# First expert's 128 rows placed by their ranks, both of its passes ahead of the sorted tiles; last token tile routed from plain rows; weighted sum at the end by diagonal matrices

## The reference

```python
x = x + gate1 * (jnp.concatenate([y_ssm, y_g], axis=-1) @ lp['w_out'])
h2 = _rmsnorm(x, lp['norm2_w']) * (1.0 + scale2) + shift2
moe_out = _moe(h2.reshape(-1, D_MODEL), router_w, router_b, lp['w_gate'], lp['w_up'], lp['w_down'])
x = x + gate2 * moe_out.reshape(x.shape)
y = _rmsnorm(x, final_norm_w)
```

## Time and profile before

| what | value |
|---|---|
| median of three runs (lowest, highest) | 549.62 us (546.81, 556.56) |
| the profiled execution | 547.45 us |
| its span | 545.7 us |
| TensorE busy | 470.6 us (86%) |
| VectorE busy | 238.7 us (44%) |
| ScalarE busy | 147.9 us (27%) |
| GpSimd busy | 102.3 us (19%) |
| moved by DMA | 164.62 MB, mean 302 GB/s |
| mean granted TensorE clock | 0.949 |

### The profile page before, as it was taken

How to read it: one execution, slowest core, us unless ns; L and a number is a source line. 1 busy time by engine, 2 the same in 40 slices (tenths; PEclk the granted TensorE clock), 3 DMA queues, 4 the chain that set the end, 5 groups by cost and what they waited for, 6 DMA issues and landing times. The chain is left out here.

```text
span 545.7 us, 8907 instructions
## 1 busy us (share of the span) xinstructions
PE 470.6 (86%) x3241; PEld 230.4 (42%) x3242; DVE 238.7 (44%) x589; ACT 147.9 (27%) x284; POOL 102.3 (19%) x182
## 2 busy tenths in 40 slices
PE   2788989899969999982888999999998999999960
PEld 1125669655559644462352333233333333333320
DVE  2698994999963300766664101111011101111067
ACT  3545794532147610231030010100001100111242
POOL 3000150988870203500500000000000000000400
PEclk9977999999999999985799999999999999999995
DMA  8992046449497999110797999999999999999922
GB/s 286 340 401 98 1 154 216 165 166 343 140 390 290 347 410 415 73 70 1 272 415 284 380 422 386 392 420 417 418 421 419 407 416 420 417 420 421 409 89 115
DMA packets 42475, 164.62 MB, mean 302 GB/s; under 512 B 3242, under 2 KB 4010, under 8 KB 32580
## 3 DMA queue, kind: packets, MB, share of 16 engines
q1 hardware_dynamic: 35440, 144.22, 67.3%
q10 hardware_dynamic: 4580, 11.91, 5.6%
q0 software_dynamic: 2416, 7.98, 3.8%
HBM read 152.76 MB, written 11.34 MB: 301 GB/s over the span
## 5 line engine op out<-in xcount | busy, mean ns | idle before, releaser
L728 PE MATMUL psum<-arena 128*64 128x512 f32 x672 | 149.1, 595 | 14.0 <-PEq L760 11.0
L728 PEld LDWEIGHTS psum<-arena 128*64 128x64 f32 x672 | 49.7, 137 | 99.5 <-issue 95.0
L741 PE MATMUL psum<-arena 128*64 128x512 f32 x336 | 76.1, 593 | 1.9 <-DVE arena L1594 1.6
L1589 DVE TENSOR_TENSOR arena<-arena,psum 128x256 f32<-128x256 f32 x21 | 8.8, 421 | 140.0 <-ACT arena L1056 140.0
L1862 POOL DMA_INDIRECT arena<-sorted_outputs,src_u x6 | 5.7, 951 | 243.8 <-DMA sorted_outputs<-arena 242.3
L741 PEld LDWEIGHTS psum<-arena 128*64 128x64 f32 x336 | 25.9, 137 | 48.0 <-issue 47.5
L656 PE MATMUL psum<-arena 128*128 128x512 f32 x96 | 41.6, 593 | 0.0
L1056 ACT ACTIVATE arena<-psum 128x256 f32<-128x256 f32 x21 | 8.0, 383 | 121.4 <-PE psum L728 121.4
L1076 ACT ACTIVATE arena<-psum 128x512 f32<-128x512 f32 x19 | 11.3, 597 | 59.8 <-PE psum L741 59.8
L656 PEld LDWEIGHTS psum<-arena 128*128 128x128 f32 x96 | 18.1, 190 | 22.1 <-issue 21.8
L1584 DVE COPY arena<-arena 128x512 f32 (+1 forms) x32 | 13.5, 423 | 30.8 <-DVEq L1602 24.8
(11 more groups left out here) (337 smaller groups left out, 645.8 us busy)
## 6 DMA issues: line engine op xcount, KB each, us to landing
arena<-in_w_gate SPq DMA_DIRECT2D x32, 1024.0 KB, 13.4
arena<-in_w_up SPq DMA_DIRECT2D x32, 1024.0 KB, 16.3
arena<-in_w_down SPq DMA_DIRECT2D x16, 2048.0 KB, 14.5
arena<-in_w_mod SPq DMA_DIRECT2D x12, 2048.0 KB, 12.5
arena<-in_w_in SPq DMA_DIRECT2D x3, 2048.0 KB, 21.5
sorted_outputs<-arena ACTq DMA_DIRECT2D x38, 128.0 KB, 6.7
arena<-in_w_out SPq DMA_DIRECT2D x2, 2048.0 KB, 17.2
arena<-modulation_rows ACTq DMA_DIRECT2D x4, 1024.0 KB, 10.5
```

Of the source, the lines that this page charges most:

```text
L728: last = mm(bank[0][HALF * t:HALF * t + HALF, :], xs[:, side, k, :], gu[:, :, k, t * 256:t * 256 + 256], start=(k == 0), stop=(k == KD - 1))
L741: last = mm(bank[4][HALF * h:HALF * h + HALF, :], hiddenT[:, s * P + t * HALF:s * P + t * HALF + HALF], dn[:, 2 * t + s, h * 512:h * 512 + ...
```

## The change

**Router.** For tile 2 TensorE transposes X itself, not h2, as soon as X is there. The norm's row factors go into the router's weights instead: `scaled_w` is router_w times (1 + scale2) * norm2_w along the channels, the result is multiplied by the reciprocal root of each token, and shift2 @ router_w is added (`shifted`). For these, GpSimd loads three small vectors, TensorE transposes them once behind the first out half and does eight products of 16 columns before the fourth; VectorE does two copies, one product and, before the second Exp, one instruction on 128x16.

**Placing.** Expert 0 always starts at position 0, so `places` is made from the ranks alone, ahead of the order of experts, and for 128 rows in two lots: one VectorE instruction on three columns and six comparisons. TensorE gathers each lot with 6 products of 512 columns; ScalarE copies both lots; both are transposed and staged.

**Order.** TensorE, ScalarE and VectorE do both passes of expert 0 before the six sorted tiles. In the loop over experts, the rest of an expert stands at the end of the step before. SP's order and its waits are as before.

**End.** For tiles 1 and 2, ScalarE makes four diagonal matrices of the weights (`weights`), and TensorE adds the gathered rows to the late parts with four products of 512 columns a tile (128 rows and columns). VectorE's `join` and one of its three instructions of `finish` go for these tiles, and the last scaling of tile 0 comes before the finish of tile 2.

The core of the diff:

```diff
             for n in range(6):
                 t, h = divmod(n, 2)
+                if n == 1:
+                    pe.wait_ge(S("columns_copied"), 1)
+                    pe.wait_ge(S("tri_done"), 2)
+                    tr(bank[3][:, P:P + 2 * KD], affine_rows[0:2 * KD, :], ident[0:2 * KD, 0:2 * KD]).then_inc(
+                        S("columns_ready"), 1)
+                if n == 3:
+                    pe.wait_ge(S("rw_in"), 80)
+                    pe.wait_ge(S("columns_copied"), 2)
+                    for k in range(KD):
+                        last = mm(bank[3][:, P + 32:P + 32 + NE], b2T[:, k:k + 1].broadcast_to([P, P]), router_w[:, k, :],
+                                  start=(k == 0), stop=(k == KD - 1))
+                    last.then_inc(S("columns_ready"), 1)
                 if n == 5:
-                    pe.wait_ge(S("states_copied"), 1)
+                    pe.wait_ge(S("columns_copied"), 3)
                     h2_columns(0, 2)
                 out_part(t, h, 0).then_inc(S("wo_ready"), 1)
-            pe.wait_ge(S("rw_in"), 32)
             pe.wait_ge(S("x1_done"), 4)
             h2_columns(1, 4)
-            route(0)
-            route(1)
-            h2_columns(2, 2)
-            route(2).then_inc(S("logits_ready"), 1)
+            route(0, router_w)
+            x_last_columns()
+            route(1, router_w).then_inc(S("logits_ready"), 1)
+            route(2, scaled_w).then_inc(S("logits_ready"), 1)
...
+            for lot in range(2):
+                pe.wait_ge(S("placed"), lot + 1)
+                for t in range(NT):
                     for h in range(2):
-                        k = 4 * h + 2 * b
-                        last = mm(bank[2 + 3 * b][HALF * h:HALF * h + HALF, 0:256], places[:, t, :],
-                                  h2[:, t, :].rearrange("p (q k) -> p k q", k=KD)[:, k:k + 2, :],
+                        last = mm(bank[(2, 5)[lot]][HALF * h:HALF * h + HALF, :], places[lot][:, t, :],
+                                  h2[:, t, :].rearrange("p (q k) -> p q k", k=KD)[:, :, 4 * h:4 * h + 4],
                                   start=(t == 0), stop=(t == NT - 1))
-            last.then_inc(S("first_ready"), 1)
-            pe.wait_ge(S("first_held"), 2)
-            for kk in range(4):
-                last = tr(bank[1 - kk // 2][:, kk % 2 * P:kk % 2 * P + P], first_rows[:, kk * P:kk * P + P], ident[:, :])
-            last.then_inc(S("first_ready"), 1)
+                last.then_inc(S("first_ready"), 1)
+            for lot in range(2):
+                pe.wait_ge(S("first_held"), lot + 1)
+                for kk in range(4):
+                    last = tr(bank[((1, 0), (7, 6))[lot][kk // 2]][:, kk % 2 * P:kk % 2 * P + P],
+                              first_rows[lot].rearrange("p (q k) -> p k q", k=4)[:, kk, :], ident[:, :])
+                last.then_inc(S("first_ready"), 1)
             pe.wait_ge(S("first_staged"), 1)
             gate_up(0, 0, 1)
-            sorted_columns(0)
             transposes(0)
-            for t in range(1, 6):
+            pe.wait_ge(S("int_done"), 1)
+            pe.wait_ge(S("first_staged"), 2)
+            pe.wait_ge(S("x_staged"), 2)
+            first_n = pe.value_load(n_i[0:1, 0:1], min_val=0, max_val=NT * P)
+            with pe.If(first_n > HALF):
+                second_pass(0, 0, 0)
+            for t in range(6):
                 sorted_columns(t)
-            pe.wait_ge(S("int_done"), 1)
             pe.wait_ge(S("hs_copied_a"), 6)
             pe.wait_ge(S("hs_copied_v"), 6)
+            with pe.If(first_n > HALF):
+                later_passes(0, 0, 0, first_n)
+            with pe.Else():
+                skipped(0, 1)
...
                     e = i * SETS + j
-                    expert_rest(j, e, i)
-                    gate_up((j + 1) % SETS, turn(0, e + 1), i + (j + 1) // SETS + 1)
+                    use = i + (j + 1) // SETS
+                    gate_up((j + 1) % SETS, turn(0, e + 1), use + 1)
                     down(j, i + 1, turn(PASSES, e), turn(PASSES - 1, e))
                     transposes(turn(0, e + 1))
+                    expert_rest((j + 1) % SETS, e + 1, use)
...
-            for part in range(2):
-                for t in range(NT):
+            pe.wait_ge(S("late_copied"), 3 + 2 * (NT - 1))
+            for t in range(NT):
+                for part in range(3):
+                    if t == 0 and part == 2:
+                        pe.wait_ge(S("last_held"), 1)
                     for h in range(2):
-                        late_part(part, t, h)
-            pe.wait_ge(S("last_held"), 1)
-            for t in range(NT):
-                for h in range(2):
-                    last = late_part(2, t, h)
+                        last = late_part(part, t, h)
+                if t > 0:
+                    pe.wait_ge(S(f"picked_in{t}"), 32)
+                    for k in range(2):
+                        for h in range(2):
+                            last = mm(late_bank(t)[:, h, :], weights[:, t - 1, k, :],
+                                      picked[:, t, k, h * 512:h * 512 + 512], start=False, stop=(k == 1))
                 last.then_inc(S("late_added"), 1)
...
-            act.wait_ge(S("int_done"), 1)
             act.sem_inc(S("evacuated"), 1)
             act.sem_inc(S("written"), 32)
             act.wait_ge(S("pad_sent"), 48)
+            gate(0)
...
+            add_out(0)
+            dve.wait_ge(S("columns_ready"), 2)
+            d(cp(view(columns_at, 2 * KD), bank[3][:, P:P + 2 * KD]))
+            d.settle()
+            tt(scaled_w, router_w, a2T.unsqueeze(2).broadcast_to([P, KD, NE]), ALU.mult).then_inc(S("columns_copied"), 1)
...
+            dve.wait_ge(S("columns_ready"), 3)
+            cp(shifted, bank[3][:, P + 32:P + 32 + NE]).then_inc(S("columns_copied"), 1)
...
+            stt(r1[:, 2, :], bank[6][:, 2 * NE:3 * NE], st[:, 8:9], shifted, ALU.mult, ALU.add).then_inc(
+                S("last_logits"), 1)
...
+            v(stt(ranked, bank[3][:, 0:NT * NE].rearrange("p (t e) -> p t e", t=NT)[:, :, 0], 1.0, mk[:, :, 0],
+                  ALU.add, ALU.mult))
+            for lot in range(2):
+                for t in range(NT):
+                    last = ts(places[lot][:, t, :], counted_rows[lot], ranked[:, t:t + 1], None, ALU.is_equal)
+                last.then_inc(S("placed"), 1)
...
-            spot = g1.rearrange(flat)
-            for t in range(NT):
-                d(ts(places[:, t, :], count_row, spot[:, t:t + 1], None, ALU.is_equal))
-            d.settle()
-            for t in range(NT):
-                last = stt(places[:, t, :], count_row, spot[:, 3 + t:4 + t], places[:, t, :], ALU.is_equal, ALU.add)
-            last.then_inc(S("placed"), 1)
...
-            for t in range(1, 6):
-                sorted_copy(t)
-            dve.wait_ge(S("hs_copied_a"), 6)
-            dve.wait_ge(S("hs_copied_v"), 6)
-            dve.wait_ge(S("pad_done"), 1)
...
+            first_n = dve.value_load(n_i[0:1, 0:1], min_val=0, max_val=NT * P)
+            with dve.If(first_n > HALF):
+                turn_over(turn(1, 0))
             matrices(1)
             matrices(2)
             matrices(0)
             dve.sem_inc(S("onehots_done"), 1)
+            with dve.If(first_n > HALF):
+                multiply(turn(1, 0))
+            for t in range(6):
+                sorted_copy(t)
+            dve.wait_ge(S("hs_copied_a"), 6)
+            dve.wait_ge(S("hs_copied_v"), 6)
+            dve.wait_ge(S("pad_done"), 1)
+            with dve.If(first_n > HALF):
...
             with dve.Fori(0, NE - 1) as e:
-                expert_rest(e)
                 to_next(e)
...
+                expert_rest(e + 1)
...
+                g2 = g2rows[:, min(t, 1), :]
+                if t == 0:
+                    dve.wait_ge(S("finish_step"), 1)
+                    tt(y2, y2, late_bank(t), ALU.add).then_inc(S("finish_step"), 1)
+                    dve.wait_ge(S("finish_step"), 2)
+                    tt(y, y, g2, ALU.mult).then_inc(S("finish_step"), 1)
+                else:
+                    tt(y2, late_bank(t), g2.rearrange("p (h c) -> p h c", h=2), ALU.mult).then_inc(S("finish_step"), 1)
+                dve.wait_ge(S("finish_step"), n)
                 tt(X[:, t, :], X[:, t, :], y, ALU.add).then_inc(S("x2_done"), 1)
...
+            turn_over(turn(PASSES, LAST))
+            dve.wait_ge(S("weighed"), 1)
+            stt(picked[:, 0, 0, :], picked[:, 0, 1, :], wts[:, 3:4], picked[:, 0, 0, :],
+                ALU.mult, ALU.add).then_inc(S("finish_step"), 1)
+            dve.wait_ge(S("g2_in"), 16)
+            finish(0, 3)
+            finish(1, 4)
+            dve.wait_ge(S("fnw_in"), 16)
+            scale_rows(0)
+            finish(2, 5)
+            scale_rows(1)
+            scale_rows(2)
...
+            for i, m in enumerate((4, 3)):
+                pool.wait_ge(S(f"modd_in{m}"), 16)
+                pool.dma_start(affine_rows[KD * i:KD * i + KD, :],
```

(2 more changed lines are left out.)

283 lines of the change are left out of this document (134 added, 149 removed).

## The result

The changed kernel takes 546.62 us in the median of 20 runs (542.97 to 547.97); the kernel before takes 550.81 in 20 runs of the same measurement (546.72 to 558.50). Leaving out the runs over 1.5% above the fastest of their kernel, two of before, the ratio is 0.9937 with a 95% interval of 0.9920 to 0.9954. That is some 3.5 us faster (2.5 to 4.4), a gain clear of the noise but well under 2%. I had forecast 1.3 us slower. The profiled execution took 545.84 us (span 544.1), 1.6 less than that of before; I had expected 548.8.

A forecast was written before the change was run, and what follows sets the result against it. Until 507 us the loads (their start and holes) were taken to bound the kernel, then TensorE and VectorE in turn; +1.7 + 1.5 - 1.9 = +1.3 us on 548.5 gave 549.8 us, range 545.0 to 556.0.

The forecast's parts named there:

- the hole in the loads: SP's queue running dry before set 2's late up and down: 9.8 us instead of 3.9, loads 5.9 us behind.
- the company of other queues: At the last loads: ScalarE's transfers and the gathers share the DMA engines, +1.5 us, bounds 0 and 3.
- The base: Time of the kernel before, taken as 548.5 us, the middle of four executions.
- Router: First VectorE instruction behind the second Exp at 247.7 us, 1.0 earlier; bounds 1.6 earlier and 1.7 later.
- First pass: Expert 0's first pass, after placing and gathering two lots, starts at 264.5 us, 3.0 ahead of 267.48.
- Second pass and sorted tiles: Expert 0's second pass, then six tiles, end at 292.9 us; set 2's up and down issued 11 us later.
- Net of the loads: Larger hole less 4.2 us of small holes that close: last up half 1.7 us later, bounds 0 and 5.9.
- TensorE's lead of 2.1 us: TensorE begins expert 1's pass at 295.6 instead of 297.73 us; the lead is spent waiting for the last loads.
- the gathers beside the last down: Part of the company term: gathers of 3 MB come 2 us earlier and share with the last down half.
- Tail: From the last down's end (D) to the last scaling: D + 20.9 instead of D + 22.8, 1.9 us shorter.
- Rival A: The loads keep up, small holes close and the tail still gains: 546.6 us, at best 543.9; chance 0.2.

The follow-up runs named there:

- wider_hole: The changed kernel with set 2's up and down issued only once the x of expert 1's first pass is staged; 551.48 us (1.0027 of before).
- after_again: The changed kernel unaltered, run and profiled a second time; 546.13 us (0.9936 of before).
- before_again: The kernel before unchanged, run and profiled again; 549.60 us (0.9999 of before).
- early_reload: The changed kernel with expert 3's gate and up issued ahead of set 2's up and down, expert 0's skipped passes counted earlier; 545.39 us (0.9907 of before).
- early_late_stage: early_reload's edit on the changed kernel, plus ScalarE's two 1.5 MB transfers moved later and VectorE reading expert 1's row before the sorted tiles; 543.72 us (0.9889).
- tail_only: The kernel before with nothing but the new end (diagonal matrices, tile by tile); 546.35 us (0.9932 of before).
- no_tail: The changed kernel with the old end; 546.16 us (0.9923 of before).
- tiles_first: The changed kernel with the six sorted tiles put back ahead of expert 0's second pass; 544.88 us (0.9897 of before).

## Why the prediction was wrong

The sum said 1.3 us slower, and the kernel is some 3.5 faster. Two of its terms failed: the hole in the loads and what it nets to (+1.7, measured near nothing), and the company of other queues (+1.5, which before pays as well). The base was off too. The steps, one by one:

- **Router**: the first instruction behind the second Exp at 247.16, forecast 247.7. The last two `route` calls take 5.57 us together, 1.65 more than the 1.96 that I had taken for each; a slow one stood only in the bound. Right within the bounds.
- **First pass**: 263.50, forecast 264.5. The gather of both lots takes 8.27 us, against 6.1 + 2.7.
- **Second pass and sorted tiles, the first step that failed.** From the first to the second pass 9.2 us instead of 9.9 (reading the count and branching leave 0.67 us idle, where I had priced 1.3 from a gap that held a copy too), from there to the end of the tiles 17.25 instead of 18.5. With the 1.0 of the first pass this is 3 us: `hs_ready` 12 at 289.96 and not 292.9. Three prices were high, by 1.0, 0.7 and 1.25 us, and their errors added up, since all stand in one chain. wider_hole puts the issue at 292.78, and the time is 551.5, 1.5 us above its before by the ratio, where I had forecast +1.3: a late issue does delay the last load and the end, and the term had the wrong size. That the two figures agree so well is partly luck, since 1.7 us of the 551.5 are the fallen clock, which my sum did not have.
- **Net of the loads, "+1.7", the step that fails by this.** Measured -0.3 in the profile (the last up half at 507.1; +0.9 in after_again, with before_again itself 1.6 above the first profile of before), since the hole is 6.2 and 5.0 us and not 9.8, and the small holes closed as I said. TensorE waits 0.8 and 1.8 us at the last expert, not 3 to 5. I subtracted large and small holes linearly. The runs speak for a threshold instead: without the hole (early_reload, early_late_stage) nothing is won, since small holes come back, while 2.4 to 3.6 us more of it (wider_hole) land the last half 2.5 to 3.6 us later. Three sizes of hole carry this, not a curve.
- **TensorE's lead of 2.1 us**, which I took to last to the end. It is 2.4 us at expert 2 (306.88 for 309.27) and 0.85 at the last expert (502.61 for 503.46). The new order of the loop costs it: at four jumps back TensorE is idle for 1.03 to 1.05 us where before had 0.65 to 0.70. My sum had no term for this.
- **Company of other queues, "+1.5"**: measured 0 as a difference. From 503 to 508 us the two queues have 52.8% (SP's) and 47.1% (ScalarE's) of the engines, as the earlier trace rows. The company is real, 2.4 to 2.8 us of landing time in the changed kernel, but before pays it as well: the last load takes 25.0 us in the earlier trace rows and 26.9 in before_again, 26.0 and 26.4 in the changed kernel. I charged a cost that both kernels have to one of them, by an argument on which transfer comes first that the earlier trace rows could not bear. The other half of the term, the gathers beside the last down, cost nothing: no down product waits for a load in either trace. The Trainium skill's rule of turns ("DMA: Bandwidth & Descriptors", Queues, rings and completion order) held in both kernels alike, and so gave no difference.
- **Tail, "-1.9"**: D + 20.9, forecast D + 20.9. Right in its parts too (0.9 and 0.45 us a product, TensorE setting the end), and all that I had left standing on the side of a gain.
- **The base.** I took 548.5 for the kernel before from four executions; 20 runs give 550.8. The first profile showed the mild case of the wait at the end (0.3 us, full clock), both later profiles of the old order with the company in place (before_again and tail_only) the other (2.1 and 2.3 us, and 1.7 us more by the clock). Ends of the last down: 519.9, 523.1, 522.2 with the old kernel up to there and the company, 520.1, 521.1, 518.7 and 520.0 for the changed kernel (two profiles), no_tail and tiles_first. The means are 521.7 and 520.0, 1.7 apart, and with the tail's 1.9 this makes 3.6 for the 3.5 measured. Seven profiles with 1 to 3 us between them carry this only as an estimate.

Rival A had the outcome: the loads keep up, 546.6. I gave it 0.2, since the rate had nothing left, and did not see that it didn't need more rate, only a hole 3.6 us smaller. That its 546.6 is the measured time is luck in part: it is 1.9 us off a base of 548.5, and the kernel gained some 3.5 on a base of 550. What stays open: whether the order of passes gains anything, why tail_only and no_tail each give about as much as both together, and how much of before's spread is the clock.

## What to carry to other kernels

Where two chains run side by side at the same pace (here 15.0 us of loads for each expert, 6.3 MB at 420 GB/s, and 15.06 of TensorE, from 306.88 to 502.61 for thirteen), a small delay in one can cost nothing and a larger one nearly all that it is larger (here 6.2 and 8.6 us): find the threshold by widening the delay, before adding or subtracting its parts. Ask of every cost that you book to a change whether the kernel before pays it too. And look at several executions of before when the last wait is one that can tip TensorE's clock: one profile shows one side of it.
